# Stick-breaking attention on one core: the meta keys of all eight heads gathered into one tile behind the last head

## The chip, the cores and the metric

The kernel runs on one core of a Trainium2 chip. The metric is the device time of one launch in microseconds (us). Below, PE is TensorE, ACT is ScalarE, DVE is VectorE, POOL is GpSimd and SP is the queue that issues most of the transfers.

## What is computed

Two layers of a gated block (its own mixing and grouped-query attention) come first and are not touched. Then comes one layer of a second block over 16 "meta" tokens followed by the 512 tokens of the sequence. It projects the normalised tokens with one wide matrix, runs two attentions, gates both and merges them. The change concerns the first of the two, the stick-breaking attention of 8 heads with 64 channels each:

```python
z = einsum('bqhd,bkhd->bhqk', q, k[:, :end]) * scale      # every earlier key, meta keys too
mask = (s < t) & valid
log_beta = log_sigmoid(z)
log_1m = where(mask, log_beta - z, 0.0)                   # = -softplus(z)
rev = cumsum(log_1m, axis=3, reverse=True)
suffix = concatenate([rev[..., 1:], 0])                   # sum over all later keys
w = where(mask, exp(log_beta + suffix), 0.0)
out = einsum('bhqk,bkhd->bqhd', w, v[:, :end])
...
y_sb = (o_sb * silu(sb_z)) @ w_branch_sb
```

So the weight of a key is the exponential of its score minus the softplus of the scores of itself and of all keys between it and the query. The meta keys are the earliest ones: their weights need the sum over all 512 later keys, and nothing else needs the meta keys.

## The kernel before

**Arithmetic.** Everything is float32 with matmuls in the rounded type fp32r, so each factor is kept as a high and a low part (`whi`/`wlo`, `hhi`/`hlo`, ...), and one product is three matmuls (`product`, lines 1526 to 1528: high x high, low x high or high x low, and the other). ACT writes the high part (`copy`, line 748), DVE the low part (`low`, lines 1285 and 1286).

**Weights.** The wide matrix comes in slabs of 1024 x 256 (`SLABS2`). SP loads one into `raw`, ACT rounds it (`split2`, line 742) and POOL subtracts (`split2_lo`, line 491), two buffers of each. PE waits for a slab in `slab2_here`; ACT rounds slab j once all units of slab j-2 are done (`UNITS_BY_SLAB2`). A "unit" is one block of output: `tokens(j, t, ...)` gives 128 tokens x 256 columns by 24 matmuls of 256 columns; `columns(j, half, ...)` gives 128 columns of the slab x all 512 tokens by 24 matmuls of 512 columns; `meta_tokens` gives the 16 meta tokens x 256 columns.

**The stick-breaking stage** (about 549 to 733 us). The order of every engine is written out by hand. Queries and keys of head pairs are projected by `qk_unit(i)`, i = 0 to 7, even ones queries, odd ones keys; an odd one first projects the 16 meta tokens against the same 128 columns, 24 matmuls of 16 columns. Units 0, 2 and 1 run ahead of head 0, and unit 3+h inside head h for h < 5. Per head h, PE runs:

- `stick_sums(h)`: with triangles and ones as stationary operand (`tri`, `ones_`), it adds the suffix sums of softplus onto the scores in PSUM, for the high and the low part: 10 matmuls on the 512 keys (line 1799), 4 that sum all keys for the 16 meta keys (line 1802, 16 output rows), and 1 for the meta keys among themselves (line 1804);
- `stick_scores(h + 1)`: scores of the next head, ending with two matmuls for its 16 meta keys (lines 1788, 1789);
- a projection that fills the time: a `qk_unit`, a `gate_unit` (h = 4, 5) or two units of slab 8 (h = 6, 7);
- `stick_values(h)`: weights times values, 3 matmuls for the meta keys (contraction over 16 rows, `vsm`) and 12 for the others (`vsb`), all into one PSUM bank.

Meanwhile ACT turns scores into softplus terms (`stick_terms`: Abs, Exp, Ln; `terms_hi`) and sums into weights (Exp, lines 823, 824); DVE does `stick_softplus`, `terms_lo`, the split of the weights (`wr`) and `sb_read`, which gates a head's output and, behind each odd head, splits the pair into `ysb`. Each of these has a piece of 16 rows x 512 for the meta keys beside the 128 x 1280 of the rest.

**Behind it** (733 to about 790 us) PE makes units of slabs 9 to 12 (`tokens`) into PSUM banks that ACT copies to `tokw`, DVE applies the rotary turn to them (`rotate`, lines 1391 to 1394), and then eight units `columns(13 + c // 2, ...)` follow whose tanh gate goes through ACT (line 879) and DVE (line 1426). The first unit of slab 9 waits for the copy of bank 0, and that copy waited for `ysb_ready` 4 (the last split of `sb_read`).

Of the kernel before, what the change touches and what calls it, by code (L numbers as in the profile page):

```python
# [17 lines left out]
CONSTS = 912  # L18
# [29 lines left out]
for i in range(2):  # L48
    SLABS2 += [("w_in_2", SB_Q + 256 * i, 8), ("w_in_2", SB_K + 256 * i, 8), ("w_in_2", SB_Z + 256 * i, 8)]
# [7 lines left out]
QK_UNIT = [11, 13, 12, 16, 17, 18, 19, 20]  # L57
QK_PLACE = [0, 2, 1, 3, 4, 5, 6, 7]
GATE_UNIT = [14, 15, 21, 22]

UNITS_BY_SLAB2 = [7, 10, 12, 16, 15, 19, 20, 22, 27, 31, 35, 39, 43] + [45 + 2 * i for i in range(20)] + \
                 [87, 91, 98, 99]
# [20 lines left out]
def build(nc, a, out):  # L83
    with ExitStack() as ctx:
# [74 lines left out]
        at[0] = base2  # L159
        ysb = sb("ysb", [P, 2, 4, SEQ], F32R)  # L160
        consts_r = sb("consts_r", [P, CONSTS], F32R)
        hm = sb("hm", [P, 2, KT, META], F32R)
# [3 lines left out]
        sb_start = at[0]  # L166
        vsb = sb("vsb", [P, 2, NT, SEQ], F32R)
        vsm = sb("vsm", [META, 2, SEQ], F32R)
        qsb = sb("qsb", [P, 4, 2, SEQ], F32R)
        ksb = sb("ksb", [P, 4, SEQ + META], F32R)  # L170
        gate_sb = sb("gate_sb", [P, 4, SEQ])
        sp_ = sb("sp", [P, 2, Z_ALL + SEQ])
        spr = sb("spr", [P, 2, Z_ALL + SEQ], F32R)
        wr = sb("wr", [P, 2, Z_ALL + SEQ], F32R)
        yb2 = sb("yb2", [P, SEQ], F32, r_sbias)
        at[0] = sb_start
# [35 lines left out]
        def qk_banks(i):  # L212
            return (4 + i, 7) if i < 3 else (stick_bank(i - 3, 0), stick_bank(i - 3, 1))


        PIECES = [(META, Z_ALL, Z_ALL + SEQ), (P, 0, Z_ALL // 2), (P, Z_ALL // 2, Z_ALL)]

        def scores(h, piece):
            rows, a0, a1 = PIECES[piece]
            if piece == 0:  # L220
                return ps[0:META, stick_bank(h, 3), :]
            b = stick_bank(h, 0)
            return ps[:, b:b + 3, :].rearrange("p b n -> p (b n)")[:, a0:a1]

        def piece_of(ap, piece):
            rows, a0, a1 = PIECES[piece]
            return ap[0:rows, a0:a1]

        GATE_BANK = [4, 5, stick_bank(4, 2), stick_bank(5, 0)]
# [5 lines left out]
        mask_sb, mask_sw, mask_sw0 = consts_r[:, 384:512], consts_r[:, 512:768], consts_r[:, 768:912]  # L235
# [288 lines left out]
        def _(act):  # L524
# [265 lines left out]
            for i in (0, 2, 1):  # L790
                qk_parts(i)
                if i == 2:
                    split2(4)
# [1267 lines left out]
```

## Time and profile before

| | us |
|---|---|
| median of 3 runs | 1126.18 (1125.09 to 1133.72) |
| the profiled execution | 1125.22 |
| its span, first to last instruction | 1123.4 |
| TensorE busy in it | 1050.4 (94%) |
| VectorE, ScalarE, GpSimd busy | 660.3, 479.8, 251.8 |

The profile is a record of one execution. Its durations of matmuls are latencies of pipelined instructions, so they overlap; what a matmul costs is read from the distance between the starts of neighbours. All sums in the prediction are made against the profiled execution.

### The profile page before, as it was taken

The page shows a single profiled execution, that of the slowest core. Times are in us where ns is not written, and L with a number is a line of the kernel's source. Part 1 is how long each engine was busy: PE and PEld are TensorE (multiplying, and loading weights), DVE is VectorE, ACT ScalarE, POOL GpSimd, SP SyncE. Part 2 cuts the span into 40 slices and gives each one's busy share as a digit, 9 for nine tenths or more (in the row PEclk, how much of TensorE's full clock was granted, in tenths as well). Part 3 has the DMA queues.
Part 4 walks back from the last instruction along what each step waited for, and adds up shares of the span by engine and source line. Part 5 has one row for each costly group of instructions (what it writes and reads, how often), then busy time and mean ns, then how long its engine had stood idle before and what let it go on. Part 6 is the DMA issues. An engine that isn't in the chain of part 4 may idle for free.

```text
span 1123.4 us, 16742 instructions
## 1 busy us (share of the span) xinstructions
PE 1050.4 (94%) x6437; PEld 916.5 (82%) x6437; DVE 660.3 (59%) x1068; ACT 479.8 (43%) x858; POOL 251.8 (22%) x167
## 2 busy tenths in 40 slices
PE   5999988999999889998989999999989988999996
PEld 5998777799998777898878777889867766888896
DVE  4667778827777778737235675577357785123203
ACT  4445444424436444334457576333355553212221
POOL 1216000002225000011313012134332342243232
PEclk9999999999999999999999999999998999999999
DMA  7323001232423001332211011122310011332311
GB/s 250 115 90 113 20 20 38 85 105 68 135 75 113 20 20 38 113 105 95 75 38 44 32 39 38 38 76 76 113 56 2 1 38 57 102 105 65 128 52 75
DMA packets 79778, 80.51 MB, mean 72 GB/s; under 512 B 5440, under 2 KB 77248, under 8 KB 79696
## 3 DMA queue, kind: packets, MB, share of 16 engines
q1 hardware_dynamic: 78080, 77.04, 21.8%
q10 hardware_dynamic: 1616, 2.36, 0.6%
q8 instruction: 53, 0.87, 0.3%
q14 instruction: 29, 0.24, 0.1%
HBM read 77.30 MB, written 2.10 MB: 71 GB/s over the span
## 4 chain that ended last, share of the span: by engine, by line
PE 67%; issue 16%; DVE 11%; ACT 5%; POOL 1%; DMA 1%; DVEq 0%; SPq 0%; POOLq 0%; ACTq 0%
PE ps L1526 18%; PE ps L1528 17%; PE ps L1527 17%; PE ps L1799 2%; PE ps L1562 2%; PE ps L1560 2%; PE ps L1561 2%; ACT pw L909 2%; DVE pwt L1285 2%; DVE small L1463 1%; PE ps L1802 1%; PE ps L1663 1%; DVE wlo L989 1%; DMA raw<-in_w_in 1%; PE ps L1616 1%
## 5 line engine op out<-in xcount | busy, mean ns | idle before, releaser
L491 POOL TENSOR_TENSOR wlo<-raw,whi 128x2048 fp32r<-128x2048 f32 (+1 forms) x31 | 136.0, 4388 | 349.3 <-ACT whi L742 349.3
L1526 PE MATMUL ps<-whi,hhi 128*128 128x256 f32 x544 | 157.3, 289 | 7.3 <-DVE hlo L980 4.3
L1527 PE MATMUL ps<-wlo,hhi 128*128 128x256 f32 x544 | 155.8, 286 | 0.0
L1528 PE MATMUL ps<-whi,hlo 128*128 128x256 f32 x544 | 155.7, 286 | 0.0
L1526 PE MATMUL ps<-hhi,whi 128*128 128x512 f32 x288 | 115.3, 400 | 2.5 <-ACT tg L924 1.7
L1527 PE MATMUL ps<-hlo,whi 128*128 128x512 f32 x288 | 114.0, 396 | 0.0
L1528 PE MATMUL ps<-hhi,wlo 128*128 128x512 f32 x288 | 114.0, 396 | 0.0
L1526 PEld LDWEIGHTS ps<-whi,hhi 128*128 128x128 f32 x544 | 106.2, 195 | 9.1 <-issue 5.2
L742 ACT ACTIVATE whi<-raw 128x2048 fp32r<-128x2048 f32 (+1 forms) x35 | 63.4, 1813 | 102.2 <-PE ps L1528 102.1
L1527 PEld LDWEIGHTS ps<-wlo,hhi 128*128 128x128 f32 x544 | 106.4, 196 | 0.0
L1528 PEld LDWEIGHTS ps<-whi,hlo 128*128 128x128 f32 x544 | 106.3, 195 | 0.0
L989 DVE TENSOR_TENSOR wlo<-raw,whi 128x2048 fp32r<-128x2048 f32 (+1 forms) x34 | 75.0, 2206 | 47.4 <-ACT whi L535 46.7
L535 ACT ACTIVATE whi<-raw 128x2048 fp32r<-128x2048 f32 (+1 forms) x34 | 61.7, 1816 | 88.2 <-PE ps L1528 84.7
L1560 PE MATMUL ps<-hhi,whi 128*128 128x512 f32 x192 | 78.1, 407 | 2.1 <-DVE wlo L989 2.1
L1562 PE MATMUL ps<-hhi,wlo 128*128 128x512 f32 x192 | 75.3, 392 | 0.0
L1561 PE MATMUL ps<-hlo,whi 128*128 128x512 f32 x192 | 75.0, 390 | 0.0
L648 ACT ACTIVATE prob<-ps,small 128x512 f32<-128x512 f32 x64 | 43.6, 687 | 64.6 <-DVE small L1183 64.5
L1526 PEld LDWEIGHTS ps<-hhi,whi 128*128 128x128 f32 x288 | 55.4, 192 | 14.4 <-issue 2.3
L1528 PEld LDWEIGHTS ps<-hhi,wlo 128*128 128x128 f32 x288 | 55.0, 191 | 11.8
L1527 PEld LDWEIGHTS ps<-hlo,whi 128*128 128x128 f32 x288 | 55.3, 192 | 11.0
L477 POOL TENSOR_TENSOR small<-small 128x4 f32<-128x4 f32 x2 | 0.4, 204 | 264.2 <-ACT junk L703 264.2
L1183 DVE TENSOR_REDUCE small<-ps 128x1 f32<-128x512 f32 x64 | 41.2, 686 | 31.0 <-PE ps L1616 30.7
(291 smaller groups left out, 2631.0 us busy)
## 6 DMA issues: line engine op xcount, KB each, us to landing
raw<-in_w_in SPq DMA_DIRECT2D x45, 1024.0 KB, 5.4
raw<-in_w_out SPq DMA_DIRECT2D x12, 1024.0 KB, 5.0
raw<-in_w_branch_swa SPq DMA_DIRECT2D x4, 1024.0 KB, 5.1
raw<-in_w_in SPq DMA_DIRECT2D x4, 512.0 KB, 3.9
raw<-in_w_branch_sb SPq DMA_DIRECT2D x4, 512.0 KB, 3.4
out<-x SPq DMA_DIRECT2D x4, 512.0 KB, 2.6
x<-in_x ACTq DMA_DIRECT2D x3, 512.0 KB, 7.2
ws<-in_spatial_w SPq DMA_DIRECT2D x2, 512.0 KB, 6.9
```

Source lines behind the costliest of these rows:

```text
L491: pool.tensor_tensor(wlo[s][:, 0:n, :], raw[s][:, 0:n, :], whi[s][:, 0:n, :].bitcast(F32), ALU.subtract).then_inc(slab_split, 1)
L535: act.activation(whi[s][:, :, 0:w], raw[s][:, :, 0:w], ACT.Copy).then_inc(whi_done, 1)
L648: act.activation(prob[:, t, :], ps[:, n % 3, :], ACT.Exp, bias=nmax[:, m:m + 1], accum_out=psum_e[:, m:m + 1]).then_inc(exp_done, 1)
L742: act.activation(whi[s][:, 0:n, :], raw[s][:, 0:n, :], ACT.Copy).then_inc(whi_done, 1)
L989: dve.tensor_tensor(wlo[s][:, :, 0:w], raw[s][:, :, 0:w], whi[s][:, :, 0:w].bitcast(F32), ALU.subtract).then_inc(slab_split, 1)
L1183: dve.reduce_max(nmax[:, m:m + 1], ps[:, n % 3, :], AX.X, negate=True).then_inc(nm_ready, 1)
L1526: pe.matmul(out_ap, lhsT=lhi(k), rhs=rhi(k), start=first and k == 0, stop=False, skip_group_check=True)
L1527: pe.matmul(out_ap, lhsT=lhi(k), rhs=rlo(k), start=False, stop=False, skip_group_check=True)
L1528: m = pe.matmul(out_ap, lhsT=llo(k), rhs=rhi(k), start=False, stop=last and k == n - 1, skip_group_check=True)
L1560: pe.matmul(ps[:, bank, :], lhsT=wh, rhs=hhi[:, k, :], start=k == 0, stop=False)
L1561: pe.matmul(ps[:, bank, :], lhsT=wh, rhs=hlo[:, k, :], start=False, stop=False)
L1562: m = pe.matmul(ps[:, bank, :], lhsT=wl, rhs=hhi[:, k, :], start=False, stop=k == KT - 1)
```

## The change

All meta keys of the eight heads become the rows of one tile: row 16h + m is meta key m of head h. Its scores gather in one PSUM bank (`META_BANK`, 7) and its sums over the later keys in another (`SUM_BANK`, 3) while the heads run, and softplus, own sums, exponential and values of that tile are done once, behind head 7.

- The meta tokens are held eight times over (`hm` is 128 columns wide instead of 16), so that `meta_tokens` gives 128 rows; a mask (`rows_of`) then keeps for row group h only head h's columns. Meta values are made so in the two units that were there; meta keys by two new calls `meta_tokens(2, ...)` and `meta_tokens(6, ...)` of 24 matmuls with 256 columns each, masked on DVE and turned on PE by two transposes each (`meta_keys_turned`) into `kmp`. The 16-column products in the key units are gone.
- `qk_unit(i)` runs in the order 1, 3, 0, 2 ahead of head 0, and 4 + h inside head h for h < 4. Keys come first, so the slabs are in another order and `UNITS_BY_SLAB2` is counted anew.
- `stick_sums` signals (`z_summed`) behind its 20 matmuls on the 512 keys; 8 more add the meta sums with a 128-column stationary `meta_keys(ones_meta, h)`. `stick_scores` signals (`z_made`) ahead of its two meta matmuls. `stick_values` has only its 12 matmuls.
- `sb_read` only gates, into `ymain`. A new `stick_out(c)` adds the gated meta part and splits into `ysb`; DVE does it between the rotary turns of the first half of slab 10's tokens. Behind the units of slab 9, PE runs `stick_meta_values`: 12 matmuls of 512 columns.
- ACT's copy of bank 0 waits for `sbo_done` 8 (head 7's values) instead of `ysb_ready` 4.
- The inverse root of the meta tokens' norm is taken by POOL in two instructions (add, pow) instead of by DVE in twelve.

```diff
@@ PE: one head @@
                         for j in range(NT - 1, to - 1, -1):
-                            pe.matmul(z_cols(h, to, j), ...)
-                    for j in range(NT):
-                        pe.matmul(meta_z(h)[:, P * j:], lhsT=ones_[:, 0:META], rhs=terms(j), ...)
-                    m = pe.matmul(meta_z(h), lhsT=tri[0:META, 0:META], rhs=spr[0:META, part, Z_ALL:], ...)
-                m.then_inc(z_summed, 1)
+                            m = pe.matmul(z_cols(h, to, j), ...)
+                m.then_inc(z_summed, 1)
+                for part in range(2):
+                    terms = lambda j: spr[:, part, Z_AT[j]:Z_AT[j] + Z_WIDTH[j]]
                     for j in range(NT):
+                        pe.matmul(ps[:, SUM_BANK, P * j:], lhsT=meta_keys(ones_meta, h), rhs=terms(j), ...)
...
-                pe.matmul(meta_z(h), lhsT=ksb[:, slot, SEQ:], rhs=qsb[:, slot, 0, :], start=True, stop=False)
-                pe.matmul(meta_z(h), lhsT=ksb[:, slot, SEQ:], rhs=qsb[:, slot, 1, :], start=False, stop=True)\
-                  .then_inc(z_scored, 1)
+                m.then_inc(z_made, 1)
+                for part in range(2):
+                    m = pe.matmul(ps[:, META_BANK, :], lhsT=kmp[:, h, :], rhs=qsb[:, slot, part, :], ...)
+                m.then_inc(z_scored, 1)
@@ PE: ahead of head 0, behind head 7 @@
-            for i in (0, 2, 1):
-                qk_unit(i)
+            qk_unit(1)
+            qk_unit(3)
+            pe.wait_ge(sv_lo, 4)
+            meta_tokens(2, meta_key_tokens(0))
+            qk_unit(0)
+            meta_keys_turned(0)
+            qk_unit(2)
...
+            pe.wait_ge(sprm_lo, 1)
+            for part in range(2):
+                m = pe.matmul(ps[:, SUM_BANK, :], lhsT=tri_meta, rhs=sprm[:, part, :], ...)
+            m.then_inc(meta_summed, 1)
+            def stick_meta_values():
+                pe.wait_ge(wrm_lo, 1)
+                for c in range(4):
+                    product(ps[:, 4 + c, :], lambda k: vsm[:, 0, c, :], lambda k: vsm[:, 1, c, :],
+                            lambda k: wrm[:, 0, :], lambda k: wrm[:, 1, :], 1).then_inc(metao_done, 1)
@@ ACT: behind head 7 @@
+            act.wait_ge(z_scored, 8)
+            copy(zraw[:], zm).then_inc(zraw_copied, 1)
+            link(act.activation(spm[:], zm, ACT.Abs))
+            link(act.activation(spm[:], spm[:], ACT.Exp, scale=-1.0))
+            act.activation(spm[:], spm[:], ACT.Ln, bias=1.0).then_inc(ln_meta, 1)
+            act.wait_ge(sp_meta, 1)
+            copy(sprm[:, 0, :], spm[:]).then_inc(sprm_hi, 1)
+            act.wait_ge(sbo_done, 8)
@@ DVE: among the rotary turns @@
+            def stick_out(c):
+                dve.wait_ge(metao_done, c + 1)
+                link(dve.scalar_tensor_tensor(yb2[:], ps[:, 4 + c, :], 0.5, gate_sb[:, c, :], ALU.mult, ALU.mult))
+                link(dve.tensor_tensor(yb2[:], ymain[:, c, :], yb2[:], ALU.add))
+                split(ysb[:, 0, c, :], ysb[:, 1, c, :], yb2[:]).then_inc(ysb_ready, 1)
+                dve.wait_ge(ysb_ready, c + 1)
```

**Where instructions move.** On PE, the end of one part of `stick_sums` and the start of the next before the change (`spr` holds softplus terms, `consts_r` the triangles and ones):

```order
L1799 MATMUL ps<-spr,consts_r 128x128
L1802 MATMUL ps<-spr,consts_r 16x512
L1802 MATMUL ps<-spr,consts_r 16x384
L1802 MATMUL ps<-spr,consts_r 16x256
L1802 MATMUL ps<-spr,consts_r 16x128
L1804 MATMUL ps<-spr,consts_r 16x512
L1799 MATMUL ps<-spr,consts_r 128x128
```

In the changed kernel the two rounds on the 512 keys stand together and the meta sums behind both; the row of 16 x 512 is gone from every head. Behind head 7, ACT's row before the change goes from the last exponential straight to the copies of slab 8's units:

```order
L823 ACTIVATE sp<-ps 16x512
L824 ACTIVATE sp<-ps 128x1280
L748 ACTIVATE tokw<-ps 128x2x256 x2
L748 ACTIVATE tokm<-ps 16x256
```

In the changed kernel the same engine has this there (`zraw`, `spm`, `sprm` are the tile of all meta keys: raw scores, softplus, its high part; `whi_53` is slab 10):

```order
L775 ACTIVATE zraw<-ps 128x512
L870 ACTIVATE spm<-ps 128x512
L871 ACTIVATE spm<-spm 128x512
L872 ACTIVATE spm<-spm 128x512
L775 ACTIVATE sprm<-spm 128x512
L775 ACTIVATE tokw<-ps 128x2x256 x2
L775 ACTIVATE tokm<-ps 16x256
L883 ACTIVATE spm<-spm 128x512
L769 ACTIVATE whi_53<-raw_51 128x2048
```

Five instructions now stand ahead of the copies, and one that waits for the finished sums stands ahead of slab 10's rounding. On DVE the four splits into `ysb` have left the heads and stand, with two instructions more each, between the rotary turns; one period of the changed kernel:

```order
L1439 SCALAR_TENSOR_TENSOR yb_109<-ps,gate_sb 128x512
L1440 TENSOR_TENSOR yb_109<-ymain,yb_109 128x512
L991 CAST ysb<-yb_109 128x512
L992 TENSOR_TENSOR ysb<-yb_109,ysb 128x512
L1459 TENSOR_TENSOR rot_114<-tokw,rope 128x8x32 x2
L1461 TENSOR_TENSOR rot_113<-tokw,rope 128x512
L1462 TENSOR_TENSOR tokw<-rot_113,rot_114 128x512
```

The upper four rows are new at this place; the lower three were there.

## Rows read from the trace of the kernel before

**Rows 1.** The page, part 1: busy time, share of the span, instructions.
```profile
PE 1050.4 (94%) x6437; PEld 916.5 (82%) x6437; DVE 660.3 (59%) x1068; ACT 479.8 (43%) x858; POOL 251.8 (22%) x167
```

**Rows 2.** TensorE by stretches: length, busy (instructions), granted clock, DMA share, GB/s.
```profile
571.50:575.30 3.80, 3.76 (x14) 0.56 0.70 240
...
593.20:606.00 12.80, 12.80 (x65) 0.87 0.00 1
...
623.20:643.10 19.90, 19.89 (x107) 0.91 0.00 1
...
549.30:733.50 184.20, 176.78 (x979) 0.97 0.15 46
```

**Rows 3.** TensorE in order of time, head 2 to 3: start, length, engine, instruction.
```profile
640.20 0.49 PE L1526 MATMUL ps<-wr,vsm 16*128 16x512 f32 x1
...
641.09 0.33 PE L1526 MATMUL ps<-wr,vsb 128*128 128x128 f32 x1
...
643.10 1.49 PE L1799 MATMUL ps<-spr,consts_r 128*128 128x128 f32 x10
644.43 0.74 PE L1802 MATMUL ps<-spr,consts_r 128*16 128x512 f32 x4
645.10 0.40 PE L1804 MATMUL ps<-spr,consts_r 16*16 16x512 f32 x1
645.43 1.60 PE L1799 MATMUL ps<-spr,consts_r 128*128 128x128 f32 x10
...
647.86 0.50 PE L1784 MATMUL ps<-qsb,ksb 128*128 128x512 f32 x1
...
650.09 0.39 PE L1526 MATMUL ps<-hhi,whi 128*128 128x512 f32 x1
```

**Rows 4.** TensorE: 24 products of 16 columns; then two gate units, 48 matmuls of 512 columns.
```profile
560.21 0.17 PE L1526 MATMUL ps<-hm,whi 128*128 128x16 f32 x1
...
562.80 0.48 PE L1526 MATMUL ps<-hhi,whi 128*128 128x512 f32 x1
...
575.32 0.43 PE L1526 MATMUL ps<-hhi,whi 128*128 128x512 f32 x1
...
586.26 1.48 PE L1799 MATMUL ps<-spr,consts_r 128*128 128x128 f32 x10
```

**Rows 5.** TensorE: three starts behind a wait, in brackets [idle before, releaser].
```profile
532.95 0.64 PE L1736 MATMUL ps<-ident,meta_row 16*128 16x16 f32 x8 [2.15 <-DVE meta_row L1292]
...
571.54 0.50 PE L1784 MATMUL ps<-qsb,ksb 128*128 128x512 f32 x1 [3.02 <-DVE ksb L1285]
...
733.49 0.36 PE L1526 MATMUL ps<-whi,hhi 128*128 128x256 f32 x1 [2.75 <-ACT tokw L748]
```

**Rows 6.** ScalarE in order of time, terms of head 4.
```profile
650.78 1.21 ACT L803 ACTIVATE sp<-ps 128x1280 f32<-128x1280 f32 x1
...
652.56 1.25 ACT L805 ACTIVATE sp<-sp 128x1280 f32<-128x1280 f32 x1
```

**Rows 7.** VectorE in order of time.
```profile
612.65 3.40 DVE L1363 CAST wr<-sp 16x512 fp32r<-16x512 f32 x1 [5.65 <-ACT sp L824]
...
654.51 2.19 DVE L1348 SCALAR_TENSOR_TENSOR sp<-ps,sp 16x512 f32<-16x512 f32 x3 [1.42 <-ACT sp L807]
656.62 2.14 DVE L1285 TENSOR_TENSOR spr<-sp,spr 16x512 fp32r<-16x512 f32 x3
...
731.96 0.69 DVE L966 TENSOR_TENSOR ysb<-yb,ysb 128x512 fp32r<-128x512 f32 x1
...
771.89 3.70 DVE L1391 TENSOR_TENSOR rot<-tokw,rope 128x256 f32<-128x256 f32 x2 [7.34 <-ACT tokw L748]
```

**Rows 8.** GpSimd in order of time: two slabs one behind the other.
```profile
606.60 9.16 POOL L491 TENSOR_TENSOR wlo<-raw,whi 128x2048 fp32r<-128x2048 f32 x2 [37.19 <-ACT whi L742]
```

**Rows 9.** Groups of weight loads by form: count | busy us, mean ns | idle before.
```profile
L1799 PEld LDWEIGHTS ps<-spr,consts_r 128*128 128x128 f32 x160 | 22.8, 189 | 5.8 <-DVE spr L1285 2.8 <-issue 1.9
...
L1802 PEld LDWEIGHTS ps<-spr,consts_r 128*16 128x16 f32 x64 | 5.5, 94 | 3.5
```

More of the change, by code:

```diff
@@ L757, in _ @@
                 copy(vsb[:, 0, t, :], ps[:, t, :]).then_inc(sv_hi, 1)
-            unit(10)
-            copy(vsm[:, 0, :], ps[0:META, 6, :]).then_inc(sv_hi, 1)
             split2(3)
@@ L790, in _, with meta_keys_hi @@
-            for i in (0, 2, 1):
-                qk_parts(i)
-                if i == 2:
-                    split2(4)
-            main, meta = slice(0, Z_ALL), slice(Z_ALL, Z_ALL + SEQ)
+                            last = copy(qsb[64 * half:64 * half + 64, 2 * (c % 2) + e, 0, :], ps[r, f, :], HD ** -0.5)
+                    else:
+                        last = copy(ksb[r, 2 * (c % 2) + e, :], ps[r, f, :])
+                last.then_inc(qk_hi, 1)
+            def meta_keys_hi(n):
+                act.wait_ge(kt_done, n + 1)
+                for e in range(2):
+                    r = slice(64 * e, 64 * e + 64)
+                    last = copy(kmp[r, 4 * n + e:4 * n + 4:2, :], meta_key_columns(n)[r])
+                last.then_inc(km_hi, 1)
@@ L796, in stick_terms @@
+            qk_parts(1)
+            qk_parts(3)
+            split2(4)
+            qk_parts(0)
+            meta_keys_hi(0)
+            qk_parts(2)
+            split2(5)
             def stick_terms(h):
-                v, b = sp_[:, h % 2, :], stick_bank(h, 0)
-                act.wait_ge(z_scored, h + 1)
+                v = sp_[:, h % 2, :]
+                act.wait_ge(z_made, h + 1)
                 if h >= 2:
                     act.wait_ge(w_lo, h - 1)
-                act.activation(v[0:META, meta], ps[0:META, b + 3, :], ACT.Abs).then_inc(ach, 1)
@@ L803, in stick_terms @@
-                link(act.activation(v[:, main], ps[:, b:b + 3, :].rearrange("p b n -> p (b n)")[:, main], ACT.Abs), 2)
-                act.activation(v[0:META, meta], v[0:META, meta], ACT.Exp, scale=-1.0).then_inc(ach, 1)
-                link(act.activation(v[:, main], v[:, main], ACT.Exp, scale=-1.0), 2)
-                for n in range(3):
+                link(act.activation(v, scores(h), ACT.Abs))
+                link(act.activation(v, v, ACT.Exp, scale=-1.0))
+                for n in range(2):
@@ L875, in _ @@
             for c in range(8):
-                unit(43 + c + 1)
+                unit(45 + c + 1)
                 if c >= 2:
@@ L1827, in _ @@
                     stick_scores(h + 1)
-                if h < 5:
-                    qk_unit(3 + h)
+                if h < 4:
+                    qk_unit(4 + h)
+                if h == 1:
+                    pe.wait_ge(w_exp, 2)
+                    meta_tokens(6, meta_key_tokens(1))
                 if h in (4, 5):
@@ L1839, in _ @@
                     if h == 7:
-                        meta_tokens(8, ps[0:META, 2, 0:256])
+                        pe.wait_ge(sbo_read, 7)
+                        meta_tokens(8, ps[0:META, 2, 0:256], 1)
                 stick_values(h)
+                if h == 1:
+                    meta_keys_turned(1)
+            pe.wait_ge(sprm_lo, 1)
+            for part in range(2):
+                m = pe.matmul(ps[:, SUM_BANK, :], lhsT=tri_meta, rhs=sprm[:, part, :], start=False, stop=part == 1,
+                              skip_group_check=True)
+            m.then_inc(meta_summed, 1)
[4 more added lines that the diff above has]
+                            lambda k: wrm[:, 0, :], lambda k: wrm[:, 1, :], 1).then_inc(metao_done, 1)
             for j in range(9, 13):
```

317 lines of the change are left out of this document (180 added, 137 removed).

## The prediction

> **What bounds the kernel now.** I read the page first: TensorE is busy for 1050.4 of 1123.4 us, the others for 660.3 or less [rows 1]. Next the windows: between 549.3 us (first query unit) and 733.5 us (first unit of slab 9) TensorE works 176.78 of 184.20 us [rows 2]. So this stage is set by TensorE, and an edit counts by what it takes from TensorE's row, from its waits (184.2 - 176.8 = 7.4 us) or from its clock. The windows show the clock too: mean 0.56 in a stretch of 3.80 us, 0.87 in one of 12.80, 0.91 in one of 19.90 [rows 2]. With 1.2 GHz as half speed this is 3.3 to 3.6 us at the lower level each time. Two of the three stretches begin with 24 products of only 16 columns, the other stands behind a wait of 3.02 us [rows 5]. Work that takes 1.67 us at full speed takes 3.34 there, so each costs about 1.7 us, 5.0 together. The timeline of one head then gives the prices, by the starts of neighbours [rows 3].
>
> **What leaves TensorE.**
> - The 16 x 512 matmul (line 1804): 645.10 to 645.43, 0.33 us, two in each of 8 heads [rows 3]: 5.3 us.
> - The meta part of the values: 640.20 to 641.09, 0.89 us [rows 3], 8 times: 7.1 us.
> - The 16-column products: 560.21 to 562.80, 2.59 us [rows 4], in four key units: 10.4 us.
> - The three slow stretches: 5.0 us, if what replaces their cause does not bring others.
> - The waits: 7.4 us, less those that come anew.
>
> **What stays, at another width.** The four meta sums (line 1802) take 644.43 to 645.10, 0.67 us for 1280 columns, with 16 output rows; the ten ahead of them take 1.33 us for 2560 columns, with 128 rows [rows 3]. Both are 0.52 ns a column, so I put the change from 16 to 128 rows at nothing, in the sums as in the scores and the meta values' projection. Between ends: nothing, and the whole of the longer weight load, 189 instead of 94 ns for 64 loads, 6.1 us [rows 9]. The nearest row, 128-column loads at the pace of 1.33 us for ten, says that the load lies beside the matmul in front of it.
>
> The Trainium skill (TensorE: Matmul & The Clock Gate, section LDWEIGHTS) has the time of a weight load go by its columns, whatever the rows, which speaks against filling 128 columns where 16 did. The two means agree with its direction (94 and 189 ns); were these loads exposed, the sum would end 6 us higher.
>
> **What comes to TensorE.**
> - `meta_tokens(2)` and `(6)`: 24 matmuls of 256 columns each. At least the 2.59 us of the 16-column ones, at most the 5.47 of 512 columns (575.32 to 586.26 is two units [rows 4]); by columns half of the latter, 2.74. I take 2.8, so 5.6 us.
> - Four transposes and two matmuls of the last sums: 0.4 and 0.6 us.
> - Meta values, 12 matmuls of 512 columns at 5.47/24 = 0.23: 2.8 us. They stand between slab 9 and slab 10, on the path.
>
> Together 9.4 us.
>
> **Waits that go and that come.** 3.02 us ahead of head 0's scores [rows 5]: the last unit there was a key unit whose split came late. Now the unit behind the one waited for is `qk_unit(2)`, 5.5 us. Behind unit 0's end stand ACT's four query copies, DVE's four low parts and two half-wide ones for `kmp`. With DVE's 0.69 us for 512 columns [rows 7] as the price of each on either engine this is at most 6.2 us, against 0.2 + 5.5 on TensorE: 0.5 us are left. 2.75 us ahead of slab 9 [rows 5]: the copy waited for DVE's gating and split; now it waits for the values themselves. The copy (0.6) and two handovers against the 0.6 us of last sums leave 0.4. ACT has five instructions more ahead of this copy (about 3 us), but behind the sums that free them TensorE has 1.3 + 3 x 2.8 + 2.0 us of other work. For DVE held up by POOL in the first heads, and for `sbo_read`, which now has 4.1 instead of 4.8 us of sums in front of it, I add 1.1. New waits: 2.0 us.
>
> At the start TensorE waits 2.15 us for `meta_row` [rows 5]. Twelve DVE steps of the root give way to two of POOL. The ends are nothing (POOL as slow as the twelve) and the whole 2.15 us; I take the middle, 1.1, since the scaling of `meta_row` and the handovers stay. The eightfold `hm` takes DVE two instructions of 1024 columns, 2.1 us at 0.69 for 512 less the faster cast, behind a unit of 2.8: nothing.
>
> **The pace of a head.** The gain holds only if ACT and DVE keep up. From `z_made` to the next `sp_lo`: Abs 1.21 and Exp 1.25 [rows 6], one Ln 0.7, two softplus pieces 1.5, the last copy 0.7, the last low part 0.8 (the three pieces take 2.19 and 2.14 us, of which a third is the meta piece that goes [rows 7]), handovers 0.5: 6.8 us. TensorE from there: meta scores 0.45, unit 5.5, values 2.0 (641.09 to 643.10 [rows 3]), 7.95. Slack 1.1 us in every head. A full head then takes 2.8 + 1.3 + 2.2 + 5.5 + 2.0 = 13.8 us.
>
> One row warns. At 612.65 a cast of 16 x 512, of which a neighbour of 128 rows would take under 0.69, takes 3.40 and ends as POOL's first slab does (606.60 plus half of 9.16, and the next begins) [rows 7, 8]; TensorE stood 1.06 us behind it. Four such slabs fall on four heads after the change, but the held instruction is the split of the weights, needed only behind the unit: 1.1 us, above, pays for it.
>
> The Trainium skill (SBUF — State Buffer, on the port pair that VectorE and GpSimd share) calls it an exclusive lock held for the whole instruction, against casts and operations with two SBUF inputs. The row at 612.65 agrees, with its end at the end of POOL's.
>
> **Behind the stage.** `stick_out` costs DVE four instructions of at most 0.69 us [rows 7], 2.8 us, four times: 11 us, and one POOL slab more may hold it for 4.6. DVE was idle 7.34 us between the halves [rows 7], the second half now starts 2.8 us later with TensorE, and the first reader (the third column unit, which needs the first gate) stands two units, 10.9 us [rows 4], behind the last block to be turned, of which turn and gate take some 4. 11 + 4.6 is within 7.3 + 2.8 + 6.9 = 17.0: nothing. Slab 10 is rounded some 2.5 us later, behind the wait for `meta_z`, and TensorE asks for it 2.8 us later: nothing.
>
> **The sum.** Out: 5.3 + 7.1 + 10.4 + 5.0 + 7.4 = 35.2. In: 9.4 + 2.0 = 11.4. Net 23.8, with the start 24.9. The profiled execution took 1125.2 us, so 1100.3; the median of the runs is 1.0 above it, so 1101.
>
> **Rivals.**
> 1. TensorE keeps the pace: 1101, between 1096 (no new wait and no slow stretch at the start either) and 1105. Chance 0.68.
> 2. ACT and DVE set the pace. For it: 1.1 us of slack is little, and POOL's hold has reached TensorE once already. Against: the hold is off the way now. If the chain were longer by 2 us, 0.9 us show in each of 7 heads, 6 us; if each hold shows whole, 4 x 2.4 = 10 us. Gives 1107 to 1111. Chance 0.16.
> 3. The 128-column loads are exposed: 1107. Against it the equal pace of [rows 3]. Chance 0.06.
> 4. DVE comes late out of the rotary turns: if POOL holds it twice more than assumed, 9.2 us minus the 1.4 in hand, 1109. Chance 0.07.
> 5. Slower than before: TensorE's clock. Transposes, short waits and single-matmul handovers replace the 16-column runs; if they let the clock fall to 1.2 GHz, each fall costs 1.7 us. It takes (24.9 + 5)/1.7, 18 falls, to lose all of the gain including the three that go, and 24 to be 1% slower (1137). The trace has three in 184 us. Chance 0.03.
>
> **How the numbers follow.** The likeliest is the first, 1101 us. The range 1096 to 1110 takes in rivals 3 and 4 and most of 2. This kernel's runs spread by under 1%, so 1% is about what can be told from no change: 1114.9 is the bound. Only rival 5, a part of 2 and effects that I don't see lie above: faster 0.93, same 0.05, slower 0.02.
>
> **What would show it.** In the changed profile: heads of 13.8 us by the starts of `stick_sums`; no clock under 1.00 between the first scores and slab 9; under 0.7 us of wait ahead of head 0's scores and of slab 9; eight meta sums in 1.3 us per head (2.0 if loads are exposed); TensorE idle under 0.3 us ahead of each `stick_sums` (0.9 and more if rival 2); the third column unit not waiting for its gate. I am wrong if the first unit of slab 9 starts less than 22 us ahead of its 733.49 us [rows 5]; by the sum it is 27.7, of which the meta values take 2.8 back.

## The result, and the profile after

The changed kernel takes 1096.22 us (median of 4 runs, 1094.11 to 1099.36) against 1126.32 us for the kernel before in the same comparison: ratio 0.9709, 95% interval 0.9672 to 0.9746. On 1126.3 us this is 32.8 us (28.6 to 36.9) less, and by the medians 30.1. The forecast was 24.9 us less: the direction and what brings the gain are as predicted, but the gain is larger. The median lies on the low end of the range of 1096 to 1110, and the time by the ratio, 1093.5 us, below it. To read the numbers of this section and the next: the runs of the kernel before in the four comparisons that follow come in two groups, 1123.7 to 1127.0 us at a mean granted clock of 0.982 to 0.990, and 1130.5 to 1134.0 us at 0.978 to 0.983 (25 and 28 of 53 runs, one of 2623 us left out), so its median moves between comparisons with the mix; those of the changed kernel do not split so.

The page, part 1, answers to [rows 1]; the window is the stretch from the first key unit to slab 9, columns as in [rows 2]:

```profile
PE 1027.7 (94%) x6367; PEld 912.5 (83%) x6367; DVE 654.2 (60%) x1037; ACT 465.4 (42%) x819; POOL 253.2 (23%) x169
```

```profile
549.39:704.11 154.72, 152.58 (x897) 135.45 (x895) 84.30 (x96) 93.75 (x111) 32.26 (x7) 1.00 0.17 55
```

TensorE lost 22.7 us of busy time, and the stretch went from 184.2 us at a mean clock of 0.97 to 154.7 at 1.00. Its waits, as the list of waits sums them up (engine, line, releaser: us in total, times, longest):

```profile
PE ps L1858 <- DVE ymain L1384: 1.1, 2, 0.8
PE ps L1858 <- issue: 0.6, 1, 0.6
PE ps L1875 <- DVE spr L1308: 0.3, 1, 0.3
PE ps L1596 <- ACT tokw L775: 0.3, 1, 0.3
```

One head in TensorE's timeline (start, length, engine, instruction), which answers to [rows 3], and behind it the start of slab 9 and the meta values:

```profile
661.15 2.92 PE L1875 MATMUL ps<-spr,consts_r 128*128 128x128 f32 x20
663.91 1.44 PE L1881 MATMUL ps<-spr,consts_r 128*128 128x512 f32 x8
665.18 0.45 PE L1858 MATMUL ps<-qsb,ksb 128*128 128x512 f32 x1
...
666.90 0.68 PE L1864 MATMUL ps<-qsb,kmp 128*128 128x512 f32 x2
667.42 0.40 PE L1596 MATMUL ps<-hhi,whi 128*128 128x512 f32 x1
...
672.90 0.39 PE L1596 MATMUL ps<-wr,vsb 128*128 128x512 f32 x1
...
674.76 1.48 PE L1875 MATMUL ps<-spr,consts_r 128*128 128x128 f32 x9
...
704.11 0.35 PE L1596 MATMUL ps<-whi,hhi 128*128 128x256 f32 x1 [0.26 <-ACT tokw L775]
...
715.69 0.39 PE L1596 MATMUL ps<-wrm,vsm 128*128 128x512 f32 x1
...
718.45 0.28 PE L1596 MATMUL ps<-whi,hhi 128*128 128x256 f32 x1
```

The head takes 674.76 - 661.15 = 13.61 us (forecast 13.8), the eight meta sums 1.27 (1.3), the meta values 718.45 - 715.69 = 2.76 (2.8).

**Where the stretch's time went.** I summed TensorE's timeline by kinds: from each start to the next, without the waits in brackets and without the half of each slow-clock time that the clock costs.

| us in the stretch | before | after | forecast of the difference |
|---|---|---|---|
| 16-column products | 10.37 | 0 | -10.4 |
| own sums, meta values (16 rows) | 12.43 | 0 | -12.4 |
| meta token units | 2.88 | 8.46 | +5.6 |
| transposes, last sums | 0 | 0.99 | +1.0 |
| values on the 512 keys | 16.94 | 15.08 | 0 |
| sums on the 512 keys | 22.45 | 22.12 | 0 |
| meta sums and meta scores | 14.45 | 14.66 | 0 |
| scores, columns and tokens units | 92.30 | 91.27 | 0 |
| waits | 7.25 | 2.14 | -5.4 |
| slow clock | 5.12 | 0.00 | -5.0 |
| all | 184.19 | 154.72 | -26.6 |

The difference is 29.5 instead of 26.6. Each term that the forecast priced came within 0.3 us. The surplus stands in rows that were to stay as they were: values 1.9, sums 0.3, the units and scores 1.0, less 0.2 in the meta sums and meta scores.

### The profile page after: what moved, and what is told of

Same layout as the page of the kernel before. It is cut to its first block, busy times and chain, and to the rows that moved or that the text cites. A ratio compares the mean times of both kernels' runs of the same rounds, so it can differ in the third digit from the quotient of the medians.

```text
span 1096.3 us, 16535 instructions
## 1 busy us (share of the span) xinstructions
PE 1027.7 (94%) x6367; PEld 912.5 (83%) x6367; DVE 654.2 (60%) x1037; ACT 465.4 (42%) x819; POOL 253.2 (23%) x169
## 4 chain that ended last, share of the span: by engine, by line
PE 66%; issue 17%; DVE 10%; ACT 5%; POOL 1%; DMA 1%; DVEq 0%; SPq 0%; POOLq 0%; ACTq 0%
PE ps L1596 18%; PE ps L1598 17%; PE ps L1597 17%; PE ps L1632 2%; PE ps L1630 2%; PE ps L1631 2%; ACT pw L946 2%; DVE pwt L1308 2%; PE ps L1875 1%; DVE small L1533 1%; PE ps L1733 1%; DVE wlo L1015 1%; DMA raw<-in_w_in 1%; PE ps L1686 1%; PE ps L1685 1%
## 5 line engine op out<-in xcount | busy, mean ns | idle before, releaser
L1597 PEld LDWEIGHTS ps<-hlo,whi 128*128 128x128 f32 x288 | 54.4, 189 | 10.6
```

The source lines that it names most:

```text
L1597: pe.matmul(out_ap, lhsT=lhi(k), rhs=rlo(k), start=False, stop=False, skip_group_check=True)
```

## Experiments

Beside the ratio, two things are read for each kernel: the length of the stretch from the first unit of 512 columns (where products of 16 stand first, from these) to the first unit of slab 9 in its profile, by the kinds above, and the median over its timed runs of span times mean granted clock, that is the work it would be at full clock, with what the clock cost (the span less this). The clock is listed to 0.001, so each such number is good to about 1 us. In these terms the kernel before is 1109.0 us of work with 16.9 to 20.3 lost to the clock, and the changed one 1085.1 and 10.4. The ratios are all against the kernel before, in runs of the same comparison. Where lines of an edit are left out, three dots stand for them; a `+` or `-` is against the kernel that the run starts from.

**The changed kernel again.**

> The changed kernel once more, beside the partial ones. Theory A (the surplus over the forecast is in the work and the start, so it repeats): ratio 0.970 to 0.972, some 31 to 34 us below the kernel before. Theory B (the surplus was a lucky share of slow-clock stretches outside the changed stage): ratio 0.975 to 0.978, 25 to 28 us. In its profile the stretch from the first query or key unit (549.4 us) to slab 9 should again be 154 to 155 us long with no granted clock under 1.00; if theory B holds, the stretch stays and the rest of the span moves.

Ratio 0.9719 (0.9685 to 0.9753), 1096.81 us against 1126.29. The stretch is 154.73 us long, and no kind differs from the table by over 0.1; its clock is 1.00. So theory A holds: the surplus repeats. In this profile the first unit of 512 columns starts at 546.44 us, 2.86 ahead of the kernel before. The work fell by 23.9 us, against a forecast of 19.9 (24.9 less 5.0 of clock), and the clock's cost by 6.5.

**The root of the meta tokens' norm alone.**

```diff
-            inverse_root(link, small2[0:META, 0:1], 1, 1.0 / D, META)
...
+            pool.tensor_tensor(m, m, eps_tile[0:META, 0:1], ALU.add)
+            pool.tensor_tensor(small2[0:META, 1:2], m, minus_half[0:META, 0:1], ALU.pow)
...
```

> The kernel before with one part of the change: GpSimd takes the inverse root of the meta tokens' norm in two instructions in place of VectorE's twelve. Theory A (only the wait shrinks, as forecast): 1.1 to 1.3 us faster. Theory B (the wait of 2.15 us also lets the clock fall at 534 us, and the shorter wait of 0.9 does not): 1.25 + 1.7 = 2.9 us faster, with no slow stretch behind the meta tokens' transposes. Theory C (slack later in the stage eats it): 0.

Ratio 0.9969 (0.9942 to 0.9995), 3.5 us (0.6 to 6.5); by the medians 2.0. The wait of 2.15 [rows 5] is 0.77:

```profile
533.74 0.64 PE L1743 MATMUL ps<-ident,meta_row 16*128 16x16 f32 x8 [0.77 <-DVE meta_row L1299]
```

The wait gives 1.4 us, above the middle that I took. The window from 530 to 549.3 us has a clock of 1.00 here and 0.91 before; this kernel, then the one before:

```profile
530.00:549.30 19.30, 18.53 (x156) 17.14 (x156) 5.96 (x11) 6.29 (x10) 5.50 (x3) 1.00 0.21 65
```

```profile
530.00:549.30 19.30, 17.15 (x135) 15.90 (x134) 5.78 (x20) 3.99 (x5) 4.64 (x1) 0.91 0.05 14
```

So the slow stretch behind the wait goes with it (another 1.7 us), as theory B has it; but this profile has slow stretches elsewhere (one more inside the stage, its clock cost 6.8 instead of 5.1), and the times can't tell 2.9 from 1.3. Across the profiles this stretch goes with the wait: the four other versions of the kernel before that keep the wait of 2.15 us all have it, and of the changed kernel's versions, whose wait is 0.9, none does.

**Without the 16-column products.**

```diff
-                if i % 2:
-                    columns(j, c % 2, ps[:, fm, 0:META], lambda k: hm[:, 0, k, :], lambda k: hm[:, 1, k, :])
```

> The kernel before without the 24 products of 16 columns in each of the four key units (the projection of the meta keys is left out, so scores of the meta keys are those of stale data). Theory A (price by start distances, 4 x 2.59, and two of the three slow stretches, which begin in these runs, go with them): 10.4 + 3.3 = 13.7 us faster, clock 1.00 between 590 and 730 us. Theory B (the slow stretches come from elsewhere and stay): 10.4 us, with two stretches still there. Theory C (ScalarE and VectorE cannot follow the shorter heads): under 8 us, and TensorE waits over 0.5 us ahead of its sums in heads 0, 2 and 4.

Ratio 0.9884 (0.9849 to 0.9918), 13.1 us (9.2 to 17.0); medians 10.5; work 9.9 us less. In the kernel before, two of the four runs of 24 products have a slow stretch right behind them. One of these, the run itself and what follows it:

```profile
593.20:595.80 2.60, 2.60 (x26) 2.55 (x24) 2.53 (x4) 2.29 (x4) 0.00 (x0) 1.00 0.02 6
595.80:599.30 3.50, 3.50 (x10) 2.82 (x11) 2.08 (x4) 3.47 (x6) 0.00 (x0) 0.51 0.00 0
```

Without the products both are gone; between 590 and 640 us the clock is 1.00:

```profile
590.00:640.00 50.00, 47.04 (x249) 35.88 (x248) 35.80 (x47) 35.33 (x50) 9.19 (x2) 1.00 0.14 43
```

The stage saves 3.4 us of clock; one slow stretch came anew behind the wait of 2.75 us ahead of slab 9, past the stretch's end, and takes 1.7 of it back, and TensorE's waits rose by 1.3. Theory A for the mechanism; the sizes 10.4 and 3.3 are near.

**Without the meta values.**

```diff
-                product(ps[:, stick_bank(h, 3), :], lambda k: vsm[:, 0, cc], lambda k: vsm[:, 1, cc],
-                        lambda k: wr[0:META, 0, Z_ALL:], lambda k: wr[0:META, 1, Z_ALL:], 1, last=False)
...
```

> The kernel before without the meta part of the values (three matmuls with 16 rows of contraction in each head; their share of the output is left out). Theory A (price 0.89 us a head as the start distances show, nothing else): 7.1 us faster. Theory B (going to 16 rows and back costs something in the neighbours too, 0.1 to 0.2 us a head): 8 to 9 us. Theory C (VectorE's split of the weights then ends last, and TensorE waits for it): under 5 us, with a wait ahead of the values of each head.

Ratio 1.0012 (0.9988 to 1.0035): nothing is gained. The stretch is 188.48 us long, 4.3 more. TensorE's work in it fell by 9.4 us, its waits rose from 7.25 to 12.52, and the clock's cost from 5.1 to 13.5 (by the runs, over the whole program, it rose by 6.7):

```profile
548.30:736.70 188.40, 175.93 (x954) 144.06 (x952) 102.27 (x133) 108.87 (x151) 32.16 (x7) 0.93 0.14 45
```

```profile
PE ps L1799 <- DVE spr L1285: 5.2, 4, 2.0
PE ps L1784 <- DVE ksb L1285: 3.0, 1, 3.0
PE ps L1526 <- ACT tokw L748: 2.8, 1, 2.8
PE ps L1526 <- DVE wr L1285: 1.5, 1, 1.5
```

The first and last of these are 1.1 and 0.4 us before. So in four heads TensorE now asks for the softplus terms 0.9 to 2.0 us before the chain of ScalarE and VectorE has them: with its 16-row pieces that chain had too little slack in the kernel before. Theory C holds for the time, though not for the place, since most of the new waits stand ahead of the sums and not of the values; theory B holds for the price: the work fell by 9.4, not by 7.1. Of the 8.4 us that the clock costs more, 5.1 lie in one stretch of busy TensorE that follows waits of 1.55 and 1.96 us, 2.2 us apart:

```profile
624.70:635.10 10.40, 10.40 (x39) 7.43 (x38) 6.12 (x10) 1.71 (x2) 0.00 (x0) 0.51 0.00 0
```

**Without the whole 16-row piece of a head, on all engines.**

```diff
-                    m = pe.matmul(meta_z(h), lhsT=tri[0:META, 0:META], rhs=spr[0:META, part, Z_ALL:], ...)
...
-                link(dve.tensor_copy(wr[0:META, 0, meta], v[0:META, meta]))
...
-                for n in range(3):
+                for n in range(1, 3):
```

> The kernel before with the whole 16-row piece of a head left out on every engine: TensorE's own sums and meta values, ScalarE's Abs, Exp, Ln, copy and Exp of 16 rows, VectorE's softplus, low part, cast and low part of 16 rows (the meta keys' share of the output is missing). Leaving out TensorE's meta values alone took nothing off the time: TensorE's work fell by 9, its waits rose by 5.3 and its slow-clock time by 8.4. Theory A (it was the chain of ScalarE and VectorE, with the 16-row pieces in it, that held TensorE up, and the waits let the clock fall): here the chain is some 2 us shorter and TensorE's work 13 us less (5.3 + 7.1 + 0.8), so 12 to 15 us faster, waits of at most 8 us in the stage, and slow-clock time no more than before. Theory B (any thinning of TensorE's row lets the clock fall, waits or not): 5 us or less faster, with short waits but 8 us and more of slow-clock time.

Ratio 0.9846 (0.9814 to 0.9878), 17.4 us on the 1131.35 of this comparison (13.8 to 21.0); work 15.3 us less. The stretch is 169.25 us, 14.9 shorter, with waits of 8.64 and the same 5.12 of clock. So it takes ScalarE's and VectorE's pieces to go along with TensorE's: theory A for the time. That waits were what let the clock fall in the run before this one fits, but no run shows it alone. The work in the stretch fell by 16.3 us, of which the removed matmuls are 12.4. The rest is in the neighbours. In this timeline the last matmul of a unit, the first of the values and the first meta sums are these:

```profile
635.38 0.39 PE L1523 MATMUL ps<-hhi,wlo 128*128 128x512 f32 x1
635.61 0.22 PE L1521 MATMUL ps<-wr,vsb 128*128 128x128 f32 x1
635.67 0.28 PE L1522 MATMUL ps<-wr,vsb 128*128 128x128 f32 x1
...
638.84 0.74 PE L1797 MATMUL ps<-spr,consts_r 128*16 128x512 f32 x4
639.42 1.53 PE L1794 MATMUL ps<-spr,consts_r 128*128 128x128 f32 x10
640.79 0.74 PE L1797 MATMUL ps<-spr,consts_r 128*16 128x512 f32 x4
```

The first values matmul takes 0.06 us to the next start; in the kernel before, behind the 16-row ones, it takes 641.25 - 641.09 = 0.16. The last matmul of the unit ahead of the 16-row ones takes 640.20 - 639.88 = 0.32; here, with 128-row ones behind it, it takes 635.61 - 635.38 = 0.23. The rows of the kernel before:

```profile
639.88 0.39 PE L1528 MATMUL ps<-hhi,wlo 128*128 128x512 f32 x1
640.20 0.49 PE L1526 MATMUL ps<-wr,vsm 16*128 16x512 f32 x1
...
641.09 0.33 PE L1526 MATMUL ps<-wr,vsb 128*128 128x128 f32 x1
641.25 0.28 PE L1527 MATMUL ps<-wr,vsb 128*128 128x128 f32 x1
```

The four meta sums take 0.58 us, and 0.67 ahead of the 16-row own sum [rows 3]; the second ten take 1.37, and 1.43 there [rows 3; to the next start at 646.86]. Over the stretch values, sums, meta sums and both kinds of scores are 3.2 us less than before, columns and tokens units 0.6.

**The same question from the other side: three 16-row matmuls a head put back into the changed kernel.**

```diff
+                product(ps[:, stick_bank(h, 2), :], lambda k: vsm[0:META, 0, h // 2, :],
+                        lambda k: vsm[0:META, 1, h // 2, :], lambda k: wr[0:META, 0, 0:SEQ],
+                        lambda k: wr[0:META, 1, 0:SEQ], 1)
```

> The changed kernel with three matmuls of 16 rows x 512 columns put back ahead of the values of every head (their result is overwritten by the values). Theory A (own start distances only, as the forecast priced them): 7.1 us more in the stage, values at 15.1 us. Theory B (the switch to 16 rows and back costs the neighbours too): 7.1 us for the three and 0.1 us and more a head in the first matmul of the values, 8 to 8.5 us in all. The chain of ScalarE and VectorE has only more time in either, so no wait can explain a difference.

Ratio 0.9775 (0.9733 to 0.9818), 1102.66 us. The stretch is 161.91 us, 7.2 more, with 1.1 less of waits: the work is 8.3 us more. The three are 7.12 of it, the values behind them 0.74 (15.82 for 15.08), and the columns units ahead of them 0.41. Theory B. The first of the values takes 0.34 us where a 512-column one takes 0.23:

```profile
660.06 0.39 PE L1598 MATMUL ps<-wr,vsm 16*128 16x512 f32 x1
660.38 0.50 PE L1596 MATMUL ps<-wr,vsb 128*128 128x512 f32 x1
660.72 0.39 PE L1597 MATMUL ps<-wr,vsb 128*128 128x512 f32 x1
660.95 0.39 PE L1598 MATMUL ps<-wr,vsb 128*128 128x512 f32 x1
```

**A 128-column stationary operand in the meta sums.**

```diff
-                        pe.matmul(meta_z(h)[:, P * j:], lhsT=ones_[:, 0:META], rhs=terms(j), ...)
+                        pe.matmul(ps[:, stick_bank(h, 3), P * j:], lhsT=ones_, rhs=terms(j), ...)
```

> The kernel before with a 128-column stationary operand in the four meta sums of each part (128 output rows instead of 16, the rest of the bank is written and not read). Theory A (the longer weight load lies beside the matmul ahead, as forecast): no change within 1 us, meta sums 10.5 to 10.8 us over the eight heads. Theory B (rival 3, loads exposed): up to 6.1 us slower, meta sums up to 16.9. In between, if only the loads behind narrow blocks show: 16 x 0.06 = 1 us.

Ratio 0.9987 (0.9966 to 1.0008), no change that the runs can tell. The meta sums take 11.71 us in the stretch instead of 10.79, 0.9 more, and everything else is as before:

```profile
645.29 0.80 PE L1802 MATMUL ps<-spr,consts_r 128*128 128x512 f32 x4
646.02 0.40 PE L1804 MATMUL ps<-spr,consts_r 16*16 16x512 f32 x1
```

The four take 0.73 us where they took 0.67, and the difference is all in the first, 0.29 for 0.23 to the next start: it stands behind a 128-column matmul of the sums. So neither nothing nor 6.1, but the case in between: the load shows only behind the narrow block, 16 times. The Trainium skill (TensorE: Matmul & The Clock Gate, section LDWEIGHTS) gives a load as its columns by 1.2 GHz, which for 128 is 107 ns. If the 0.06 us from a 128-column matmul to the next start here cover their part of that, some 0.05 us are left, 0.8 us in 16, an estimate by that rule; the 0.9 us of the run agree, while the profile's records of such loads, 189 ns each [rows 9], are longer than the rule has them.

**The order of wide and narrow blocks.** The change also turned the order of the values' blocks, widest first, and I had priced this at nothing without saying so.

```diff
-                for j in range(NT):
+                for j in range(NT - 1, -1, -1):
...
```

> The changed kernel with the values' blocks in the old order, the 128-column block first and the 512-column block last (the change had turned this round, which the forecast priced at nothing). In the two profiles the twelve matmuls take 16.9 us in eight heads before, 16.2 where only the meta values are left out, 15.1 in the changed kernel. Theory A (the order is worth 1.1 us and the 16-row neighbour 0.8): values take 16.2 us here, and the stage is 1.1 us longer. Theory B (the order is worth nothing, all comes from neighbours): 15.1 us, no change.

Ratio 0.9696 (0.9668 to 0.9725), 1096.21 us: no difference to the changed kernel, and the stretch is 154.69 us. The values take 15.44 instead of 15.08, but the sums behind them 21.83 instead of 22.12. The order only moves a stall over the boundary. Neither expectation of the size (16.2 or 15.1) was right; no change is theory B. The stronger form, wide and narrow in turn in sums, meta sums and values:

```diff
+                order = [todo.pop(0 if n % 2 == 0 else -1) for n in range(len(todo))]
+                for n, (part, to, j) in enumerate(order):
...
```

> The changed kernel with the matmuls of the sums, the meta sums and the values in another order: a wide block and a narrow one in turn (512, 128, 512, 128, 384, ...) instead of widths in a falling or rising run. A 128-column matmul behind a wide one took 0.06 us to the next start, behind a narrow one 0.11. Theory A (a narrow matmul is too short to hide the next weight load, and the wide ones have room): sums 22.1 to 19.5, values 15.1 to 14.2, meta sums 10.5 to 9.6 us, together 3 to 4 us faster. Theory B (the load's time shows behind every narrow matmul wherever it stands, as the turned order of the values suggested, where 0.36 us went from the values and 0.29 came to the sums): no change within 0.5 us.

Ratio 0.9707 (0.9678 to 0.9735); stretch 154.77 us, sums 22.31, values 15.46, meta sums 10.59. Nothing is gained: theory B.

**The slack of the other engines.** ScalarE's Abs once or twice more in each head:

```diff
+                link(act.activation(v, scores(h), ACT.Abs))
```

> The changed kernel with ScalarE's Abs of the scores done twice in every head, 1.24 us more in the chain from scores to sums. Theory A (the slack of the chain is 1.1 us, as forecast; in the changed kernel's profile the last low part ends at 673.65 and TensorE asks at 674.76): TensorE waits 0.1 to 0.2 us ahead of the sums in heads 1 to 7, more only where GpSimd holds VectorE; 1 to 2 us slower. Theory B (the slack is used up already, as rival 2 has it): 7 x 1.2 = 8 us slower and waits of over 1 us ahead of each head's sums. If waits let the clock fall, 1.7 us come on top for each fall.

1098.55 us, ratio 0.9709 (0.9679 to 0.9739); the stretch is 156.35 us, 1.6 more, of which 0.55 are waits and 0.85 longer distances in the values. Theory A.

With the Abs done three times:

> The changed kernel with ScalarE's Abs of the scores done three times in every head, 2.5 us more in the chain from scores to sums, against a slack of 1.1. With one more Abs the stage grew by 1.6 us, and no clock fell. Theory A (slack 1.1 us, then ScalarE sets the pace): waits of 1.4 us ahead of the sums in each of 7 heads, 10 us in all, stage 164 to 166 us. Theory B (other queues, such as the copies of the projections behind the chain, take part): 12 to 17 us. On the clock: if waits of over a microsecond are what lets it fall in this stage, slow stretches appear between 560 and 700 us, each for 1.7 us more; if only the runs of narrow products do, the clock stays 1.00 and the waits stand alone.

1107.47 us, ratio 0.9808 (0.9769 to 0.9846); the stretch is 164.59 us, 9.9 more, and the work with full clock 9.3 more. Theory A's 10 us. The waits, and the window:

```profile
PE ps L1877 <- DVE spr L1310: 7.7, 6, 1.3
```

```profile
546.30:710.80 164.50, 153.81 (x896) 135.84 (x894) 85.37 (x95) 112.82 (x127) 32.24 (x7) 1.00 0.16 51
```

Six waits of 1.1 to 1.3 us ahead of the sums, and the clock stays 1.00.

**Do the narrow runs lower the clock by themselves?**

```diff
+                if i % 2:
+                    columns(QK_SLAB[i], c % 2, ps[:, QK_BANK[i], 0:META], lambda k: hm[:, 0, k, 0, :], ...)
```

> The changed kernel with 24 products of 16 columns put back ahead of each of the four key units (their result is overwritten by the unit). Theory A (such a run lets the clock fall by itself): 10.4 us of work and 1.7 us for each slow stretch, and granted clocks under 1.00 behind the runs; 12 to 17 us slower than the changed kernel. Theory B (it takes a wait or other thin work near it, as the kernel before had ahead of its first scores): 10.4 us and a clock of 1.00 from the first key unit to slab 9.

Ratio 0.9874 (0.9826 to 0.9921), 1114.49 us, 18 above the changed kernel. The 96 products take 10.36 us, waits are 2.1, and the clock costs 6.8 us in the stretch where it cost nothing. In the timeline the four runs lie at 546.1, about 554, 613.2 and 649.7 us, and the windows behind three of them read:

```profile
554.00:564.00 10.00, 10.00 (x51) 8.55 (x50) 1.38 (x2) 1.18 (x2) 0.00 (x0) 0.83 0.34 106
610.00:630.00 20.00, 19.20 (x106) 17.09 (x105) 8.45 (x12) 6.98 (x10) 0.00 (x0) 0.83 0.00 1
645.00:660.00 15.00, 14.76 (x81) 12.85 (x80) 10.63 (x10) 7.65 (x9) 4.58 (x1) 0.89 0.24 71
```

In the first TensorE is busy for 10.00 of 10.00 us. No wait is needed: theory A. Not every run of products does it: of the 24 in the six profiles that have them in the stage, 14 have a slow stretch behind them. In the nine profiles of the changed kernel and its versions without them the clock is 1.00 from the first unit to slab 9. Over the whole program this kernel lost 17.8 us to the clock, as the kernel before does (18.0 here), and the changed kernel about 10.

**The wait for the gated read, moved behind nine matmuls.**

```diff
-                    pe.wait_ge(sbo_read, h - 1)
+                    pass
...
-                for j in range(NT):
+                for j in (0, 1, 3, 2):
+                    if j == 2 and h >= 2:
+                        pe.wait_ge(sbo_read, h - 1)
```

> The changed kernel with the wait for the gated read of the head before moved behind nine of the twelve score matmuls (only the block in the third bank needs it), blocks in the order 0, 1, 3, 2. Theory A (the waits of 0.81 and 0.24 us ahead of the scores of heads 2 and 4 are covered by the 1.4 us of matmuls that now come first): waits in the stage 1.1 instead of 2.1 us, stage 153.7 instead of 154.7. Theory B (VectorE, held by GpSimd, is later than TensorE gets there or the wait appears ahead of the values): no change. A difference of 1 us can't be told by the run times, so the profile decides.

Stretch 153.41 us, 1.3 shorter, waits 1.10: theory A. The time is 1096.11 us, ratio 0.9706 (0.9679 to 0.9733), which can't be told from the changed kernel.

**Both edits together.**

> Both edits together, as the version meant to be faster than the changed kernel. If both first theories hold: stage 154.7 - 3.5 - 1.0 = 150 us and some 1092 us in all. If only the later wait pays: 153.7. Rival: the shorter heads use up the slack of 1.1 us in the chain of ScalarE and VectorE (3.5 us over 8 heads takes 0.4 of it in each), so up to all of it stays; only where GpSimd holds VectorE would waits of 0.5 us and more come back.

Stretch 153.47 us, 1095.64 us, ratio 0.9693 (0.9665 to 0.9721): the later wait's gain alone. No version here is measurably faster than the changed kernel.

## Why the prediction was wrong in its size, and where it was right

- **TensorE sets the stage.** Right: 152.58 of 154.72 us busy, and the edit paid by what left TensorE's row.
- **What leaves: the step that failed.** The 16-column products were priced at 10.4 (10.37 in the stretch, 9.9 by the runs without them). The own sums and meta values were priced at 5.3 + 7.1 = 12.4 by their own start distances, and their neighbours at nothing. The switch to 16 rows and back costs the matmuls ahead and behind as well: 3.2 us in eight heads among values, sums and scores, and some 0.4 to 0.6 in the units. The runs show it both ways: 16.3 us of work went for 12.4 priced when all of it goes, and 8.3 came for 7.1 when a part comes back. What the chip does at such a switch is not shown.
- **What stays at another width.** Forecast nothing, between 0 and 6.1. The meta sums alone are 0.9 and the meta scores 0.5 (4.13 for 3.66). These were the second half of the same mis-sizing, of the other sign. They hid in the row of the meta sums, which in sum fell by 0.3, since a neighbour's cost of 1.2 went. The equal pace of 0.52 ns a column, from which the forecast took that width costs nothing, was luck: 0.09 of the 0.67 us belonged to the switch behind the four. Rival 3, at 6.1 us, is out. Together 3.9 less 1.4 is 2.5 of the 2.9 us by which the stretch came out shorter than forecast; the rest is not assigned.
- **What comes.** 9.4 forecast; 5.58 + 0.99 + 2.76 = 9.3.
- **Waits.** New ones 2.0 forecast, 2.14 measured, and where they were put: 0.56 ahead of head 0's scores (0.5), 0.26 ahead of slab 9 (0.4), 1.3 at the reads and sums of the first heads (1.1).
- **The clock, and the second term that was too small.** 5.0 forecast for three stretches, 5.1 measured. The windows in which they stood were read loosely: the slow stretches lie behind the runs of products and not in them, and the window of 19.90 us begins behind a wait of 1.06 us. A fourth stretch, behind the wait at 532.95 us, was left out of the sum for the start, though a window there shows it (0.91). It goes with the wait in both kernels that shorten it, another 1.7 us. The start then gives 2.9 us in the repeat (546.44 for 549.30) instead of 1.1. In the first profile of the changed kernel this was hidden, since slow stretches in the first two layers had put it 2.7 us behind by 525.9 us.
- **Pace of a head.** 13.6 for 13.8. The forecast's terms of the chain add up to 6.7 and not 6.8 us, which changes nothing. The cast of 612.65 us ends at 616.05, as GpSimd's second slab does (606.60 + 9.16 = 615.76), not its first. The chain had 1.1 us of slack as forecast: VectorE's last low parts end at 672.09 + 1.56 = 673.65 and TensorE asks at 674.76. One Abs more cost 1.6 us, two more 9.9. Rival 2 is out by that margin, and is what happens 1.4 us further on.

```profile
672.09 1.56 DVE L1308 TENSOR_TENSOR spr<-sp,spr 128x640 fp32r<-128x640 f32 x2
```

- **Behind the stage.** Nearly right, and by a hair: slab 10 is 26.6 us ahead of the kernel before at its first unit, the window stage 26.3 at its start. The missing 0.3 is rival 4 in small. GpSimd held VectorE twice while the four new groups ran, 8.7 us in all, where I had allowed 4.6, and a third time, 4.4 us, in the turns behind them. The new groups took 10.6 us for 11. VectorE's first gate then ends at 764.03 us, where TensorE, at 0.23 us a matmul, would have begun the third column unit at 763.91; it begins at 764.18. The wait is too short for the list of waits, and stands in the repeat too (0.52 us from start to start). So the margin was used up. One of the three holds, the gate, and the first matmul of the third unit with the one ahead:

```profile
743.86 5.05 DVE L1440 TENSOR_TENSOR yb<-ymain,yb 128x512 f32<-128x512 f32 x1
...
763.35 0.68 DVE L1496 SCALAR_TENSOR_TENSOR gate_sw<-tz,ps 128x512 f32<-128x512 f32 x1
...
763.68 0.39 PE L1598 MATMUL ps<-hhi,wlo 128*128 128x512 f32 x1
764.18 0.47 PE L1596 MATMUL ps<-hhi,whi 128*128 128x512 f32 x1
```

- **Slower, by the clock.** The reverse of rival 5: four transposes and short waits bring no slow stretch. Two of the three that went had stood behind narrow runs, the third behind the wait of 3.02 us, which is 0.56 now.
- **The range.** Its low end of 1096 took in no new wait and no slow stretch at the start, but no error in the prices of what goes. Stage 2.9 us more, start 1.8 more, and a clock that in most runs costs some more outside the stage before than after, make the missing 5 to 8 us. How the last part divides over the program isn't settled, since each run's profile puts the slow stretches outside the stage elsewhere.

## What to carry to other kernels

Here a matmul that used few rows cost more than the distance from its start to the next: compare its neighbours' distances with those of the same instruction elsewhere, and price both switches. Work taken off the engine that sets the pace pays only as far as the chain of the others has slack, so look for that slack first, and cut the same piece on all engines. A short run of very narrow products can cost twice, once in its own time and once in the clock of the wide work behind it. A margin that comes out at 1.4 us of 17 is worth naming as thin: here it was used up, and cost 0.3 us.

## What was not expected of the hardware

- The switch between a 16-row and a 128-row matmul takes about 0.1 us behind the run (0.16 for 0.06, 0.34 for 0.23) and about as much ahead of the next 16-row one (0.32 for 0.23, 0.67 for 0.58).
- Runs of 24 products of 16 columns, 2.6 us long with TensorE busy throughout, are followed by 3.4 or 6.8 us at a granted clock of 0.5 (1.2 instead of 2.4 GHz) in two of four places before, in three of four in the kernel that puts them back, and in 14 of 24 over all profiles. Single waits of up to 1.3 us between wide work are not followed by any in the changed kernel; two of 1.55 and 1.96 us close together, in the kernel before without its meta values, were followed by 10.2 us of it.
- Leaving out 24 matmuls of 16 rows (7.1 us of their own) raised the clock's cost there from 5.1 to 13.5 us in the profile, nearly the 9.4 us of work that went, and by 6.7 us in the median of the runs.
- The order of wide and narrow matmuls is worth nothing in sum here, in a run of either direction or in turn: the stall behind a narrow one moves with it. What sets it is not settled by these runs.
